# Draining the attention values later in VectorE's step, and the order of two small jobs ahead of the gated output

## The reference

```python
def window_ctx_attention(q, k, v, k_ctx, v_ctx, sink):
    # 8 blocks of 128 queries; each sees its own block of keys, the one before
    # and the one after (|i-j| <= 128), 256 context keys, and a sink logit per head
    s_loc = jnp.where(valid, einsum(q, k_band) * scale, NEG_INF)
    s_ctx = einsum(q, k_ctx) * scale
    p = softmax(concatenate([s_loc, s_ctx, s_sink], -1))
    return einsum(p_loc, v_band) + einsum(p_ctx, v_ctx)

def merge(y_a, o_d, z, gate_a, gate_d):
    y_d = rms_norm_2(o_d, dn_norm_g) * silu(z)      # per head of 64
    y = sigmoid(gate_a) * (y_a @ w_br_attn) + sigmoid(gate_d) * (y_d @ w_br_dn)
    return y @ w_out

x_new = x + gt1 * merge(y_attn, o_dl, dz, ga, gd)   # gt1: one factor per column
```

## Time and profile before

| | |
|---|---|
| median of 3 runs | 4033.23 us (4032.6 to 4033.34) |
| the profiled execution | 4033.23 us, of which the span of its instructions is 4031.3 us |
| PE busy in the span | 3823.5 us (95%) |
| VectorE busy in the span | 1720.5 us (43%) |
| ScalarE / GpSimd busy | 1044.0 us (26%) / 711.3 us (18%) |

### The profile page before, as it was taken

The page is one execution under the profiler, slowest core; times in us unless marked ns, Lnnn a source line. Parts: engine busy times, 40 slices in busy tenths (PEclk is TensorE's granted clock), DMA queues, the critical chain, the costliest instruction groups (busy, mean ns, idle before and its releaser), DMA issues. The chain is left out here.

```text
span 4031.3 us, 43752 instructions
## 1 busy us (share of the span) xinstructions
PE 3823.5 (95%) x17424; PEld 2635.6 (65%) x17424; DVE 1720.5 (43%) x2966; ACT 1044.0 (26%) x1774; POOL 711.3 (18%) x542
## 2 busy tenths in 40 slices
PE   8989999999999999999997899898899989999998
PEld 4455444444458888887654787755688648888886
DVE  2165775533032223234456888466821142222332
ACT  1044563000022222113242323114811022121210
POOL 1053000000001110001002021003801113333333
PEclk9999999999999999999898889699999999999999
DMA  4100102334001111111201121310012201111111
GB/s 150 39 23 5 46 3 73 104 115 146 32 32 53 42 53 52 43 58 57 115 1 20 34 40 35 108 45 1 2 47 69 89 21 53 53 43 52 53 42 53
DMA packets 200184, 211.49 MB, mean 52 GB/s; under 512 B 64560, under 2 KB 152240, under 8 KB 199600
## 3 DMA queue, kind: packets, MB, share of 16 engines
q1 hardware_dynamic: 140624, 172.50, 13.0%
q10 hardware_dynamic: 59360, 36.19, 3.4%
HBM read 185.33 MB, written 21.50 MB: 51 GB/s over the span
## 5 line engine op out<-in xcount | busy, mean ns | idle before, releaser
L95 PE MATMUL ps<-halves 128*128 128x512 f32 x7296 | 1662.7, 390 | 23.6 <-DVE halves L378 11.4
L95 PEld LDWEIGHTS ps<-halves 128*128 128x128 f32 x7296 | 1372.9, 188 | 312.0 <-DVE halves L378 11.6
L95 PE MATMUL ps<-arena 128*128 128x512 f32 (+2 forms) x3088 | 1294.9, 579 | 19.9 <-DMA arena<-in_w_in 14.3
L95 PEld LDWEIGHTS ps<-arena 128*128 128x128 f32 x3088 | 588.5, 198 | 665.1 <-issue 653.0
L1251 POOL TENSOR_TENSOR tmps<-tmps 128x512 f32<-128x512 f32 x128 | 137.4, 1074 | 1000.1 <-ACT tmps L1219 1000.1
L1272 DVE TENSOR_TENSOR halves<-tmps,halves 128x512 fp32r<-128x512 f32 x128 | 88.5, 692 | 524.1 <-ACT halves L1227 524.1
L1158 ACT ACTIVATE halves<-raws 128x2048 fp32r<-128x2048 f32 x62 | 118.4, 1909 | 559.7 <-PE ps L95 524.6
L896 POOL TENSOR_TENSOR arena<-arena 128x512 f32<-128x512 f32 x32 | 41.9, 1310 | 937.4 <-DVE arena L867 688.9
L1258 POOL TENSOR_TENSOR arena<-arena 128x512 f32<-128x512 f32 x128 | 164.7, 1294 | 191.4 <-DVE arena L1295 191.4
L1219 ACT ACTIVATE tmps<-ps 128x512 f32<-128x512 f32 x128 | 76.5, 598 | 376.9 <-PE ps L95 376.9
L1165 DVE TENSOR_TENSOR halves<-raws,halves 128x2048 fp32r<-128x2048 f32 x62 | 142.1, 2292 | 73.6 <-ACT halves L1158 73.6
(11 more groups left out here) (278 smaller groups left out, 3437.9 us busy)
## 6 DMA issues: line engine op xcount, KB each, us to landing
arena<-in_w_in SPq DMA_DIRECT2D x16, 2048.0 KB, 9.0
raws<-in_w_ff SPq DMA_DIRECT2D x31, 1024.0 KB, 5.2
raws<-in_w_mlp SPq DMA_DIRECT2D x31, 1024.0 KB, 5.2
arena<-in_w_ada ACTq DMA_DIRECT2D x24, 1024.0 KB, 5.2
arena<-in_w_out SPq DMA_DIRECT2D x4, 2048.0 KB, 10.2
mixw<-in_w_in SPq DMA_DIRECT2D x16, 512.0 KB, 4.1
h_stash<-arena SPq DMA_DIRECT2D x1, 5120.0 KB, 21.0
inverses<-arena ACTq DMA_DIRECT2D x20, 256.0 KB, 2.9
```

Of the source, the lines that this page charges most:

```text
L95: ins = e.matmul(out_ap, l, r, start=i == 0, stop=i == n - 1)
```

## The change

Three edits, all in VectorE's list:
1. In `vector_watt` the block "values" goes from the start of step i to its end, behind the scores of pair i and the reciprocals of pair i-1, ahead of "tokens". It still handles pair i-5.
2. In `vector` the call of `vector_gated_stats` stands ahead of `vector_row` instead of behind it, and the wait for the bank of `qkv` 7 in front of `vector_row` is gone.
3. `TM1` lies in the scratch that the squares of the statistics and the tanh of the gates use (Z2 + 1024, 1024 columns), instead of the place that the weights `aq` had (3072).

```diff
             for i in range(32 + 5):
-                u = i - 5
-                if 0 <= u < 32:
-                    n, j, lo, hi = watt_pair(u)
-                    key = ("wp", u)
-                    e.wait_ge(*bk.full(key))
-                    cols = slice(n * 128, n * 128 + 128)
-                    e.tensor_copy(AQH[:, j, cols], bk.tile(key)[:, 0:128]).then_inc(*dv.tick())
-                    e.wait_ge(*dv.now())
-                    e.tensor_tensor(AQL[:, j, cols], bk.tile(key)[:, 0:128], AQH[:, j, cols].bitcast(F32),
-                                    ALU.subtract).then_inc(*bk.emptying(key))
                 if i < 32:
...
                     e.reciprocal(c[:, 6:8], c[:, 2:4]).then_inc(*w_rc.tick())
+                u = i - 5
+                if 0 <= u < 32:
...
+                    e.tensor_tensor(AQL[:, j, cols], bk.tile(key)[:, 0:128], AQH[:, j, cols].bitcast(F32),
+                                    ALU.subtract).then_inc(*bk.emptying(key))
                 if i - 1 in SPLIT_AT:
                     vector_tokens_lo(e, *SPLIT_AT[i - 1])
...
-        TM1, TM2 = R3(3072, 8, 128), R3(47104, 8, 128)
+        TM1, TM2 = R3(Z2 + 1024, 8, 128), R3(47104, 8, 128)
...
             vector_qkv2(e)
-            e.wait_ge(*bk.full(("qkv", 7)))
+            vector_gated_stats(e)
             vector_row(e, 16, TM1)
-            vector_gated_stats(e)
             vector_gated(e)
             vector_watt(e)
```

More of the change, by code:

```diff
@@ L2531, in vector_watt @@
                     e.reciprocal(c[:, 6:8], c[:, 2:4]).then_inc(*w_rc.tick())
+                u = i - 5
+                if 0 <= u < 32:
+                    n, j, lo, hi = watt_pair(u)
+                    key = ("wp", u)
+                    e.wait_ge(*bk.full(key))
+                    cols = slice(n * 128, n * 128 + 128)
+                    e.tensor_copy(AQH[:, j, cols], bk.tile(key)[:, 0:128]).then_inc(*dv.tick())
+                    e.wait_ge(*dv.now())
+                    e.tensor_tensor(AQL[:, j, cols], bk.tile(key)[:, 0:128], AQH[:, j, cols].bitcast(F32),
+                                    ALU.subtract).then_inc(*bk.emptying(key))
                 if i - 1 in SPLIT_AT:
```

## The result

The changed kernel takes 4107.85 us (median of 4, 4103.83 to 4111.29) against 4032.91 us before: ratio 1.0186, 95% interval 1.0173 to 1.0199, 75 us slower. The forecast was 4124 us. The profiled execution took 4104.32 us and is one of the quicker ones.

A forecast was written before the change was run, and what follows sets the result against it. PE leads the whole kernel, but VectorE sets the pace in the middle of `watt`. Loop 53.1, clock 27 and row 10.9 sum to 91 us, on 4033.2 giving 4124 us; range 4090 to 4142.

The forecast's parts named there:

- the rival that the clock holds: In `watt`, PE's pauses leave the clock at 1.00 and the new turns cost only 53.1 us: 4097 us, chance 0.20.
- The loop: In `watt`, VectorE and PE take turns through the values' bank: 6.43 us a turn against 4.02, together +53.1 us.
- the row: Ahead of `z`, PE's row product waits for the statistics now standing ahead of the diagonal tiles: +10.9 us.
- the clock: In `watt`, PE's pause of 2.6 us in each turn lowers the granted clock in most turns: +27 us.
- the six pauses: Of seven PE pauses of 2.4 to 2.9 us in the trace, those after which the clock fell; mean 0.59 behind them.
- The rival of 24 slow turns: In `watt`, every turn runs at the low clock, costing 38 us beyond the 53.1: 4135 us, chance 0.15.
- short and long pause leave the same low clock behind: At the row product, PE leaves short pauses or one long pause at a low clock: 0, with 2 us either way.
- Nothing else moves: Behind step 31 of `watt` the last steps keep their length and VectorE's 5.7 us of waits stay.
- idle time of VectorE in each step: Sign in `watt`: VectorE's first drain of scores idles 1.7 to 3.2 us in each step from 8 to 31.
- steps with and without tokens alike: Sign in `watt`: steps 6.4 to 8 us apart, whether or not they hold tokens.
- `z` later by 11 us: Sign behind the row product: everything from the first `z` on moves by about 11 us.
- the length of `watt`: Sign: `watt` should last about 220 us instead of 140.

The follow-up runs named there:

- the second profile: The changed kernel run once more without further edits, against the kernel before, for a second look at its slow turns: 4108.26 us.

## Why the prediction was right

The 4107.85 us lie inside the stated range, 16 us under the forecast of 4124 and 11 us over the rival that the clock holds (4097): the time falls between the two, and nearer to the rival. No errors cancelled. The loop and the row were right term by term and make up 62 of the 75 us; the clock was too dear, and the range was wide enough for it.

*The loop through the bank.* Right in its mechanism, its place and its size. The prediction had a turn of 6.43 us; turns at the full clock take 6.42. It had +53.1 us for steps 5 to 31 at the full clock, and with the clock held (transposes twice) these steps show 50.2 + 1.7 = 51.9. The 1.2 us lie in the five turns with a shorter W or narrower scores (6.21 and 5.67 us), each of which adds some 0.2 us less to its old length than the others do, and which I had counted like them. That S(i+1) behind W(i) is the link is shown by the run that takes W out from between.

*The clock.* Right in kind, mis-sized: 27 us forecast, 11.6 measured. The price of a slow turn was right (8.0 us forecast, up to 8.25 measured; the seven cost 1.7 us each for the 1.6 of the sum), the number was not: 6/7 x 0.82, or 70% of the 24 turns, where 7 or 8 were slow, some 30%. I took that share from pauses of 2.4 to 2.9 us elsewhere in the program. Here PE pauses 24 times, for 1.5 to 2.6 us. Behind four of the seven slow turns the pause is only 1.5 us, behind the other three 1.8 to 2.6. Between slow turns lie up to four at the full clock, most with the same 2.59 us in front of W as the slow ones; two slow ones also follow each other (28 and 29, and 7 and 8 in the second profile). So the length of a pause alone doesn't decide, and the six pauses were a poor sample: they stood singly in other surroundings. I had also misread them. The clock had not fallen "at once" behind all six: behind the 2.69 us pause it was still 1.00 in the first us (2701.30 to 2702.30) and 0.50 only from about 2702.4 on, and behind the one of 2.56 us, at 2516.69, it was 1.00 in the first us too. And I had stopped at 2.9 us: behind a pause of 3.26 us, at 1198.93, the next 4 us show 1.00. What does decide was not settled. That they come from what PE does between the turns is shown by the transposes done twice: with more work and a shorter pause there they are gone. The rival of 24 slow turns would have cost 38 us, and is further off than my 27.

*The row and the statistics.* +10.9 forecast, +10.5 in the marks, 10.7 in the profile with this part alone (11.6 by its medians). That short and long pause leave the same low clock behind held within 0.3 us in this pair of profiles; in other profiles the stretch to the first transposes of y_d varies by about 1 us with the clock it draws (18.75 to 19.58 us with the old order, 29.27 to 30.27 with the new).

*Nothing else moves.* The tail behind step 31 is 14.95 us in both profiles. Of VectorE's 5.7 us of waits there 4.7 are left, where I had all of them stay; the tail is no shorter for it.

The error of the sum, 16 us, is the clock's term (15) and little else. The signs came in kind: idle time of VectorE in each step, steps with and without tokens alike, `z` later by 11 us. Their sizes were less good: VectorE's idle times run from 1.2 to 4.1 us and not from 1.7 to 3.2, PE's pauses from 1.5 to 2.6 and not from 2 to 2.7, and the granted clock, 0.90, is at the edge of the 0.6 to 0.9 named. I had the length of `watt` at about 220 us; it was 203.

## What to carry to other kernels

When a drain moves within an engine's step, ask first who waits for that PSUM bank and what is queued behind the waiter: a bank that is reused once a step makes the order inside the step part of a loop, and the price is the pickup by the other engine plus all that it does before the first engine's next input. Count the banks opened in a step; where the count equals the number of banks, as here, each drain has its fixed bank. With the next scores queued behind the waiter, the drain at the head of the step was hidden, in the middle it cost 0.2 us in the steps without tokens, and at the end 2.4 us a step; with the waiter moved behind those scores, the end cost nothing either, but for the tokens of the next section. Statistics that nobody waits for yet belong behind the small job that the busiest engine waits for.

## What the hardware showed beyond that

*More work, less time.* 304 needless transposes made the changed kernel about 13 us faster, 11.6 of them between the marks, as the granted clock stayed at 1.00 (2.4 GHz).

*VectorE and GpSimd stand in each other's way.* Where a tokens subtraction (both inputs in SBUF) and GpSimd's scaling overlap, the one that comes second takes longer. Before, the tokens started 0.17 us ahead (2852.05) and took 0.67 us, and GpSimd's pair, timeline of GpSimd, took longer:

```profile
2848.21 3.74 POOL L2577 TENSOR_SCALAR arena<-arena,wst 128x640 f32<-128x640 f32 x2 [0.51 <-DVE wst L2531]
2852.22 4.11 POOL L2577 TENSOR_SCALAR arena<-arena,wst 128x640 f32<-128x640 f32 x2 [0.27 <-DVE wst L2531]
```

After the change the reciprocals release GpSimd two instructions earlier, so it comes first and keeps its 3.74 us, and the tokens take 1.00 us. In the changed kernel that lay in idle time; with W behind the next scores, where VectorE has none, it was 0.33 us in each of 11 steps, the 3.6 us that were over. The Trainium skill, "SBUF — State Buffer", section "SBUF: two separate sides", says that these two engines share a pair of ports under an exclusive lock, the first to start keeping it for its whole instruction. The trace agrees that the two hinder each other and that the first isn't lengthened; the second pays 0.37 us as GpSimd and 0.33 as VectorE. It doesn't agree with the whole instruction: with W behind the next scores, the first of GpSimd's two instructions runs from 2856.75 to 2858.64, and the tokens, begun at 2857.09, are done at 2858.09, still inside it. Here the measurement decides, and a third of a microsecond is the price. That the ports are the cause was not tested by itself.

*The same program, 13 us apart.* The kernel before ran from 4024.8 to 4037.6 us in these series. Differences below 0.1% were readable only by marks on both sides of the edit.
